# A two-block transformer kernel: gate columns first in ScalarE's DMA queue, rotation angles behind the scaled input, and the gates' rows turned and spread one half earlier

## The reference, cut to what matters

```python
h = rmsnorm(x, norm1_gain[l])
(aq, ak, av, mq, mk, mv, mi, mf, mo, gate_a, gate_m) = split_columns(h @ w_in[l])
aq = partial_rope(rmsnorm(aq..., q_norm_gain[l]), positions)     # needs cos and sin of positions * inv_freq
...
i_pre = GATE_CAP * jnp.tanh((mi + ml_i_bias[l]) / GATE_CAP)      # 8 heads
f_pre = GATE_CAP * jnp.tanh((mf + ml_f_bias[l]) / GATE_CAP)
...
lfc = jax.nn.log_sigmoid(f_pre); b = jnp.cumsum(lfc, axis=-1)    # running sums over the tokens, then running maxima
hm = mlstm_chunkwise(...)                                        # weights exp(b_t - b_s + i_s - m_t)
```

## Time and profile before

| what | value |
|---|---|
| median of 3 executions | 1375.44 us (1373.81 to 1378.73) |
| the profiled execution | 1373.92 us, span of its instructions 1372.2 us |
| TensorE busy | 1200.6 us, 87% of the span |
| mean granted TensorE clock | 0.956 of full speed |
| first matmul of h0 | 15.12 us after the span's start |
| first matmul of `spread` | 58.06 us, after 5.24 us of idle TensorE |

### The profile page before, as it was taken

The page is one execution under the profiler, slowest core; times in us unless marked ns, Lnnn a source line. Parts: engine busy times, 40 slices in busy tenths (PEclk is TensorE's granted clock), DMA queues, the critical chain, the costliest instruction groups (busy, mean ns, idle before and its releaser), DMA issues.

```text
span 1372.2 us, 16858 instructions
## 1 busy us (share of the span) xinstructions
PE 1200.6 (87%) x6468; PEld 872.5 (64%) x6468; DVE 716.9 (52%) x1453; ACT 576.9 (42%) x1264; POOL 831.4 (61%) x509
## 2 busy tenths in 40 slices
PE   6899999995998778788877877787999999999998
PEld 6797899993433333233333333333999899999997
DVE  4735217257967585766758576555487413211111
ACT  6365656452423232224323232225566365544442
POOL 6656658955664545454454555441876458788885
PEclk9899999997999999999899999999999999999999
DMA  8423445629999999999999999998544335455551
GB/s 249 154 93 102 145 126 191 210 66 412 426 425 425 425 426 425 426 426 425 426 425 427 425 426 427 425 427 301 184 159 142 100 123 184 151 188 184 184 186 60
DMA packets 138417, 381.86 MB, mean 278 GB/s; under 512 B 8545, under 2 KB 99681, under 8 KB 105569
## 3 DMA queue, kind: packets, MB, share of 16 engines
q0 software_dynamic: 36864, 268.45, 46.6%
q1 hardware_dynamic: 100000, 112.25, 25.2%
q10 hardware_dynamic: 1472, 0.09, 0.1%
HBM read 379.72 MB, written 1.05 MB: 277 GB/s over the span
## 4 chain that ended last, share of the span: by engine, by line
PE 50%; DMA 30%; DVE 11%; ACT 6%; issue 2%; POOL 1%; ACTq 0%; DVEq 0%; SPq 0%
PE ps L645 30%; DMA rows_w<-peer_rows_in,arena 29%; PE ps L864 9%; PE ps L1031 4%; DVE rows_w L1890 2%; PE ps L983 2%; ACT w_hi L421 1%; DVE arena L1890 1%; DMA ring<-w_in_in 1%; ACT arena L1150 1%; ACT wgt L1314 1%; PE ps L938 1%; POOL rows_w L605 1%; PE ps L728 1%; DVE arena L1615 0%
## 5 line engine op out<-in xcount | busy, mean ns | idle before, releaser
L429 POOL TENSOR_TENSOR w_lo<-ring,w_hi 128x1024 fp32r<-128x1024 f32 x206 | 498.9, 2439 | 222.0 <-ACT w_hi L421 221.9
L864 PE MATMUL ps<-arena,diag 128*128 128x512 f32 x448 | 231.2, 668 | 86.9 <-ACT diag L1320 86.9
L864 PE MATMUL ps<-rows_w,diag 128*128 128x512 f32 x512 | 240.2, 613 | 32.6 <-ACT diag L1320 32.6
L421 ACT ACTIVATE w_hi<-ring 128x1024 fp32r<-128x1024 f32 x206 | 211.7, 1057 | 134.4 <-PE ps L645 96.2
L645 PE MATMUL ps<-hT_hi,w_hi 128*128 128x256 f32 x816 | 235.4, 288 | 7.9 <-POOL w_lo L429 7.9
L605 POOL DMA_INDIRECT arena<-peer_rows_in,arena x112 | 130.7, 1167 | 182.2 <-PE ps L864 165.0
L864 PEld LDWEIGHTS ps<-arena,diag 128*128 128x128 f32 x448 | 90.9, 211 | 224.0 <-ACT diag L1320 122.9
L645 PE MATMUL ps<-hT_lo,w_hi 128*128 128x256 f32 x816 | 232.6, 285 | 0.0
L645 PE MATMUL ps<-hT_hi,w_lo 128*128 128x256 f32 x816 | 232.4, 285 | 0.0
L605 POOL DMA_INDIRECT rows_w<-peer_rows_in,arena x128 | 165.6, 1294 | 104.1 <-PE ps L864 90.5
L1890 DVE CUSTOM_DVE_ANT_0 rows_w<-rows_w,arena 128x1024 f32<-128x1024 f32 x128 | 156.4, 1225 | 115.6 <-DMA rows_w<-peer_rows_in,arena 115.4
(11 more groups left out here) (382 smaller groups left out, 1720.1 us busy)
## 6 DMA issues: line engine op xcount, KB each, us to landing
ring<-w_in_in SPq DMA_DIRECT2D x45, 1024.0 KB, 5.1
ring<-w_ffn_gate_in SPq DMA_DIRECT2D x11, 1024.0 KB, 5.1
ring<-w_ffn_up_in SPq DMA_DIRECT2D x11, 1024.0 KB, 5.2
ring<-w_ffn_down_in SPq DMA_DIRECT2D x11, 1024.0 KB, 5.1
ring<-w_out_in SPq DMA_DIRECT2D x8, 1024.0 KB, 5.0
ring<-w_branch_attn_in SPq DMA_DIRECT2D x4, 1024.0 KB, 5.2
ring<-w_branch_mlstm_in SPq DMA_DIRECT2D x4, 1024.0 KB, 4.9
ring<-peer_w_query_in SPq DMA_DIRECT2D x4, 1024.0 KB, 4.9
```

What stands on the lines that cost most here:

```text
L421: act.activation(hi_of(n, u)[:, t, 0:cols], raw_half(n, g)[:, t, 0:cols], ACT.Copy).then_inc(sem("hi_ready"), 1)
L429: pool.tensor_tensor(lo_of(n, u)[:, t, 0:cols], raw_half(n, g)[:, t, 0:cols], hi_of(n, u)[:, t, 0:cols].bitcast(F32), ALU.subtract).then_i ...
L864: ins = pe.matmul(acc[:, c, :], diag[:, p % 4, :], pick_row(p % TOPK, D + c * CW, CW), start=False, stop=True, skip_group_check=True)
```

## The change

Four edits. (1) The gate columns' DMA is issued first in ScalarE's queue, ahead of `pos`, `freq` and `gcol`. (2) VectorE scales x before it makes the angles; these now stand between `xn1` and `hT_lo`. (3) `gate_rows` stands behind h2 on TensorE in place of h3, `spread` behind h4 in place of h5; ScalarE's parts move up by one half likewise, and `row_exp` comes ahead of `qk_root(3)`. (4) VectorE's row chain stands ahead of `qk_squares(3)` in place of behind `qk_rotate(3)`.

```diff
-        after1[3].append(("gate_rows", 0))
-        after1[5].append(("spread", 0))
+        after1[2].append(("gate_rows", 0))
+        after1[4].append(("spread", 0))
...
+            act.dma_start(raw_half(0, 0)[:, :, HALF:HALF + 2 * MH], w1[:, :, MI0:MO0]).then_inc(sem("gate_cols"), 16)
             for t, v in (("pos", pos_i[:]), ("freq", freq[:])):
                 act.dma_start(v, a[t]).then_inc(sem("pos_loaded"), 16)
             act.dma_start(gcol[:], a["gcol"]).then_inc(sem("gain_loaded"), 16)
-            act.dma_start(raw_half(0, 0)[:, :, HALF:HALF + 2 * MH], w1[:, :, MI0:MO0]).then_inc(sem("gate_cols"), 16)
...
-            act1[3].append((gate_rows, 0))
-            act1[4].append((row_exp, 0))
+            act1[2].append((gate_rows, 0))
+            act1[3].insert(0, (row_exp, 0))
             for part in range(3):
-                act1[6 + part].append((spread, part))
+                act1[5 + part].append((spread, part))
...
+            for b in range(NB):
+                dve.wait_ge(sem("r_ready"), b + 1)
+                for c in range(2):
+                    dve.tensor_scalar(xn1[:, b, c * CW:(c + 1) * CW], xres[:, b, c * CW:(c + 1) * CW], rr[:, b:b + 1], None,
+                                      ALU.mult).then_inc(sem("xn_ready"), 1)
             dve.wait_ge(sem("pos_loaded"), 2 * 16)
             link(dve.tensor_copy(posf[:], pos_i[:]))
...
-            for b in range(NB):
-                dve.wait_ge(sem("r_ready"), b + 1)
-                for c in range(2):
-                    dve.tensor_scalar(xn1[:, b, c * CW:(c + 1) * CW], xres[:, b, c * CW:(c + 1) * CW], rr[:, b:b + 1], None,
-                                      ALU.mult).then_inc(sem("xn_ready"), 1)
...
-            qk_squares(3)
-            qk_rotate(3)
             dve.wait_ge(sem("rows_gates"), 1)
...
             dve.tensor_scalar(rows[:, 4, :], rows[:, 4, :], -1.0, None, ALU.mult).then_inc(sem("m_rows"), 1)
+            qk_squares(3)
+            qk_rotate(3)
             qk_squares(4)
```

## The result

| | before | changed |
|---|---|---|
| median of 22 executions | 1375.40 us (1373.33 to 1381.11) | 1381.09 us (1375.32 to 1384.91) |
| profiled execution | 1373.92 us, span 1372.2 | 1381.59 us, span 1379.9 |

The change makes the kernel slower: 5.7 us by the medians, and a ratio of 1.0028 (3.9 us) with a 95% interval of 1.0017 to 1.0038, which is 2.3 to 5.2 us. The means, 1376.3 and 1380.1, agree with the ratio. The medians are further apart since the changed kernel's executions lie in two groups, 7 between 1375.3 and 1377.6 and 15 between 1380.0 and 1385.

A forecast was written before the change was run, and what follows sets the result against it. It took TensorE's idle at the start and in front of `spread` as the bounds. 1373.92 + 8.2 (angles) + 2.5 (slow h0) - 2.1 (gates) = 1382.5, put at 1383.0 us; range 1377 to 1388.

The forecast's parts named there:

- The angles are held: At the start, VectorE's angle instructions wait out GpSimd's subtraction pieces; h0 starts at 23.3, not 15.12: +8.2 us.
- Slow half h0: After TensorE's long idle at the start, h0 begins at the low clock: +2.5 us (bounds 1.5 and 3.5).
- The gates: Moved `gate_rows` and `spread`, counted from h2's end: gain between 0.4 and 7.3 us, taken as 2.1.
- The sum: Whole kernel: 1373.92 + 8.2 + 2.5 - 2.1 = 1382.5 us, with the forecast put at 1383.0.
- Not held: Rival at the start: angle instructions pass beside GpSimd, h0 starts at 14.4; 1366 to 1373 us, chance 0.08.
- The gates give all: Rival: angles held, but TensorE's clock stays up through waits at `gate_rows` and `spread`; 1377.3 to 1379 us, chance 0.12.
- The gates give nothing or cost: Rival: angles held and the clock falls at both waits; +10.7 to +12.7, 1385 to 1388 us, chance 0.22.
- The order of DMAs does nothing: Rival at the start: GpSimd and the angles both start 1.5 us later; 1384 us, counted with the forecast.

The follow-up runs named there:

- e4: The changed kernel with the angles' intermediate rows in PSUM, so that no angle instruction but the first works from SBUF to SBUF: 1370.62 us, ratio 0.9958.
- e1: The kernel before with edit 2 alone (x scaled first, then the angles; gate columns still last in ScalarE's DMA queue): 1376.15 us, ratio 1.0005.
- e2: The kernel before with edit 1 alone (gate columns' DMA first, angles still ahead of the scaling of x): 1380.47 us, ratio 1.0037.
- e6: The changed kernel with `gate_rows` behind h3 on TensorE as before, `spread` still behind h4: 1383.88 us, ratio 1.0053.
- e9: The changed kernel, unaltered, profiled a second time: 1377.15 us.
- e10: The changed kernel, unaltered, profiled a third time: 1381.42 us.
- e7: The changed kernel with the angles' intermediate rows in PSUM and 26 extra matmuls filling the wait in front of `spread`: 1369.70 us, ratio 0.9961.

## Why the prediction came out right

- **The angles are held** (+8.2): right in kind, shown by e4 and e1, too large by 2.2. Four were held, as forecast; measured +6.0. The gate columns land at 5.0 and not 9.6, so GpSimd starts at 9.17 and not 10.9 and runs out at 19.1 and not 20.7. And there is a gap of 0.31 us in front of h1, in which two instructions got through, so that five and not seven were left. The arbitration rule of the Trainium skill (DMA: Bandwidth & Descriptors) gave the direction of this error: columns earlier than 9.6, and a sum about 1 us lower. That arbitration is the cause no run shows; e2's columns, first as well, took 4.3 us.
- **Luck in this term.** The forecast has the angles start with `freq` at 10.6. They start at 8.90, right behind the scaling of x, and `freq` has been there since 7.3. How many are held hangs on the distance to GpSimd's start, and that was 0.3 us forecast and 0.27 measured, since both times were 1.7 us too late.
- **Slow half h0** (+2.5): measured 8.18 - 6.26 = +1.9, and 1.3 to 1.6 in e6, e9 and e10. The low clock itself stands in the record of e9 (0.52), not in that of the changed kernel's first profile. It doesn't take a long wait right in front of h0: e2 idles 0.71 us there, behind transposes that start at 15.43, and pays 2.2.
- **The gates** (-2.1): in the profiled execution the start and h0 make +7.9 by 29.3 and L667 is 7.1 late, so the gates give 0.9. The waits came as worked out: 2.88 for 2.9 at `gate_rows`, 3.20 for 3.6 at `spread`. In e9 and e10 the early fall of the clock gives another 3.2 us, counted from the end of h0, by the path that the prediction named (h3 and h4 lose what the wait would have taken). 2.1 lies between the two, and no profile shows it.
- **The sum**: +8.6 forecast, 1381.59 - 1373.92 = +7.7 in the profiled executions, +5.7 in the medians. The 2.0 between them is the choice of execution: the profiled one of the kernel before lies 1.5 under its median, that of the changed kernel 0.5 above. The sum is nearer than its terms: the start and h0 were 2.8 too large, the gates' gain 1.25 too large, and 0.6 came in behind the head that the prediction had put at nothing. The prediction set its line between slower and unchanged at 0.3%: the medians, 0.41% apart, are beyond it, and the ratio of 1.0028, with 0.28%, just is not. Its chances for slower are added up as 0.84 and make 0.86.
- **Rivals.** "Not held" falls by the rows of the changed kernel. "The gates give all" comes out in time for 7 of 22 executions, at or below its 1377.3 to 1379, but by other terms: e9 has +6.1 at the start, +1.4 for h0 and -4.1 for the gates, in place of 10.7 and -7.3, and `spread` is wholly at full speed in no profile of the changed kernel. "The gates give nothing or cost" had as its condition a clock that falls at both waits. In e9 and e10 it fell at `gate_rows` (0.73) and again within `spread`, and there the gates gave 4.1 us. "The order of DMAs does nothing" falls: it does much, and e2 shows it harmful alone. Its price of 1384 was wrong too: e1 has GpSimd at 12.44 and the old order, nothing is held, and it takes 1376.
- **Not foreseen in the prediction**: that e1's edit, the scaling of x ahead of the angles, is harmless or nearly so without the DMA edit, and that the DMA edit alone costs as much as the whole change. The prediction costed edit 1 as a small gain and put the loss under edit 2. In fact the angles are late only together with an early GpSimd.

What stays open is why e10's later stages, at the same head, take 4 us more than e9's, and why five profiles of thirteen have this longer form. The granted clock doesn't tell them apart: in the stretch of the first fetched rows, 300 to 345, it was 0.81 in e10 and 0.85 in e9, but from 350 to 600 it was 0.95 in e10 and 0.93 in e9. No experiment tested it.

## What to carry to other kernels

Before a transfer or an engine is made earlier, ask what it sets off: here the earlier gate columns started GpSimd's subtractions 3 us sooner, and a chain of tiny VectorE instructions from SBUF to SBUF then got through at one per 2.4 us piece. Put such chains where GpSimd is idle, or give them a PSUM input (e4, with the rest of the change kept: 1370.6 us, where the kernel before took 1375.7 and the changed one 1381.1). An execution's time can also be decided in two places at once, each with two outcomes: cut the profiles at fixed points before a difference of a few us is put down to the edit. A wait that moves is not a wait that goes: `spread` started when its row chain was ready, whatever TensorE did in between.

## What the runs showed of the hardware

- VectorE instructions of 8 or 16 elements from SBUF to SBUF that started while GpSimd subtracted (pieces of some 2.4 us) took 2.2 to 2.4 us, to the end of the piece; with a PSUM input at the same place they took 0.17 to 0.20 (changed kernel, e4).
- A DMA of 64 KB in pieces of 64 bytes, issued at 2.21 us as the fourth of ScalarE's queue, took 8.9 us, and 4.2 when it was issued first, at 0.81. Whether the place in the queue or the transfers beside it made the difference no run separates.
- TensorE's granted clock in e7 was 1.00 in the 3.1 us of matmuls with 128 rows, 1.00 through `spread`'s matmuls with 8 rows, and 0.53 in the 3.6 us after, with no idle time between.
- Executions of one program differ by which waits lower the clock: in the first profile the clock was 1.00 behind the 2.88 us wait at `gate_rows` and 0.50 behind the 3.20 us wait; in e9 and e10 it was 0.73 in the 6.4 us behind the wait at `gate_rows`.
